# Four projections of a hybrid decoder layer as seven half products in place of eight, with the sums of two on GpSimd

## What is computed

```python
x += W_out[concat(NSA heads, GLA heads)](RMSNorm(x) @ W_in)   # NSA: 8 query heads, 2 key/value heads, 3 branches
q = rms_norm(q.reshape(B, S, NSA_HEADS, dh), q_norm_g)        # each head of 64 is normed
q_rot = apply_partial_rope(q, positions)                      # the first 16 features of each head are turned
o = (o_intra + o_inter); o = rms_norm(o, norm_g)              # GLA: 4 heads, values of width 128
return (o * jax.nn.silu(r)).astype(q.dtype)                   # r: the GLA gate
x += MoE(RMSNorm(x))                                          # top 4 of 32 experts, 1024 -> 2048 -> 1024 each
```

## Time and profile before

| | before |
|---|---|
| median of 3 runs | 1060.35 us (1059.74 to 1060.77) |
| span of the profiled execution | 1056.8 us |
| median less span | 3.55 us |
| TensorE busy | 1015.2 us (96%) |
| VectorE, ScalarE, GpSimd busy | 311.4, 167.2, 15.8 us |
| TensorE's waits in the first 160 us | 3.3 us |
| memory read | 424.83 MB, 403 GB/s over the span |

### The profile page before, as it was taken

One profiled execution on the slowest core, in us unless ns is written; L12 is line 12 of the kernel. 1 busy time (PEld: TensorE's weight loads), 2 busy tenths in 40 slices (PEclk: granted clock), 3 DMA queues, 4 the chain that ended last, 5 costly groups with the idle time before them and its releaser, 6 DMA issues.

```text
span 1056.8 us, 12109 instructions
## 1 busy us (share of the span) xinstructions
PE 1015.2 (96%) x4965; PEld 409.4 (39%) x4965; DVE 311.4 (29%) x711; ACT 167.2 (16%) x324; POOL 15.8 (1%) x42
## 2 busy tenths in 40 slices
PE   9999999999999999999999999999999999999998
PEld 6555654333333333333233333333333333333333
DVE  1666675222212222222222222222112221222222
ACT  2433422111101111111011001111111110111111
POOL 4100000000000000000000000000000000000000
PEclk9999999999999999999999999999999999999999
DMA  9992599999999999999999999999999999999997
GB/s 293 361 381 85 215 368 378 419 426 432 431 430 429 433 433 426 433 433 433 432 429 433 434 432 429 432 434 432 429 434 433 430 429 431 431 432 429 422 424 288
DMA packets 37187, 426.37 MB, mean 403 GB/s; under 512 B 3927, under 2 KB 12207, under 8 KB 20513
## 3 DMA queue, kind: packets, MB, share of 16 engines
q1 hardware_dynamic: 35120, 424.52, 95.8%
q0 software_dynamic: 704, 1.04, 0.5%
q10 hardware_dynamic: 1328, 0.33, 0.1%
HBM read 424.83 MB, written 1.05 MB: 403 GB/s over the span
## 4 chain that ended last, share of the span: by engine, by line
PE 66%; DMA 30%; DVE 2%; issue 1%; ACT 0%; SPq 0%; DVEq 0%
PE bank L1859 26%; DMA pair<-in_w_down 26%; PE bank L1871 15%; PE bank L1426 5%; DMA pair<-in_w_gate_up 4%; PE bank L1893 4%; PE bank L1835 3%; PE bank L1701 2%; PE bank L1885 2%; PE bank L1843 1%; PE bank L1878 1%; PE bank L1498 1%; PE bank L2095 1%; PE bank L1458 1%; PE bank L1485 1%; PE bank L1468 1%
## 5 line engine op out<-in xcount | busy, mean ns | idle before, releaser
L1859 PE MATMUL bank<-pair,xs 128*64 128x512 f32 x2032 | 446.3, 594 | 20.3 <-DMA pair<-in_w_gate_up 19.2
L1859 PEld LDWEIGHTS bank<-pair,xs 128*64 128x64 f32 x2032 | 142.2, 137 | 319.1 <-issue 286.0
L1871 PE MATMUL bank<-pair,sig 128*64 128x512 f32 x960 | 212.4, 594 | 13.3 <-DMA pair<-in_w_down 13.3
L1319 DVE COPY gu<-bank 128x512 f32<-128x512 f32 x32 | 36.3, 1134 | 413.9 <-PE bank L1859 413.9
L1871 PEld LDWEIGHTS bank<-pair,sig 128*64 128x64 f32 x960 | 72.4, 137 | 149.1 <-issue 143.7
L794 ACT COPY gu<-bank 128x512 f32<-128x512 f32 x32 | 36.2, 1133 | 457.7 <-PE bank L1859 457.7
L903 DVE TENSOR_TENSOR xs<-bank,gt 128x512 f32<-128x512 f32 x31 | 21.4, 691 | 220.5 <-PE bank L1843 220.5
L1426 PE MATMUL bank<-stage,xt 128*128 128x512 f32 x160 | 72.2, 598 | 0.0
L1893 PE MATMUL bank<-ys,pgt 64*128 64x512 f32 x248 | 61.6, 615 | 0.0
L1835 PE MATMUL bank<-xr,onehot 128*64 128x512 f32 x248 | 58.5, 592 | 0.0
L799 ACT COPY ys<-bank 128x512 f32<-128x512 f32 x31 | 18.1, 585 | 206.4 <-PE bank L1871 206.4
(11 more groups left out here) (338 smaller groups left out, 524.9 us busy)
## 6 DMA issues: line engine op xcount, KB each, us to landing
pair<-in_w_gate_up SPq DMA_DIRECT2D x51, 4096.0 KB, 40.9
pair<-in_w_down SPq DMA_DIRECT2D x24, 4096.0 KB, 38.9
pair<-in_w_gate_up SPq DMA_DIRECT2D x20, 2048.0 KB, 12.8
pair<-in_w_down SPq DMA_DIRECT2D x18, 1024.0 KB, 12.2
stage<-in_w_in SPq DMA_DIRECT2D x5, 2048.0 KB, 19.0
pair<-in_w_down SPq DMA_DIRECT2D x4, 2048.0 KB, 31.0
pair<-in_w_gate_up SPq DMA_DIRECT2D x8, 1024.0 KB, 7.6
stage<-in_w_out SPq DMA_DIRECT2D x2, 2048.0 KB, 13.4
```

The lines of the kernel that those rows point to most:

```text
L1319: V.tensor_copy(gu[:, 1, :].rearrange("p (i q) -> p q i", i=FQ), up_banks[1][:].rearrange("p (q i) -> p q i", i=FQ)).then_inc(s["gu_lo"], 1)
L1859: last = mm(up_banks[a][b * CAP:(b + 1) * CAP, :].rearrange("p (q i) -> p q i", i=FQ), xs[:, k, :], cols[:, b], start=k == 0, stop=k == DK ...
L1871: last = mm(down_bank[b * CAP:(b + 1) * CAP, :], actf[:, kk % FQ, kk // FQ, :], row[:, 512 * b:512 * (b + 1)], start=kk == 0, stop=kk == D ...
```

## The change

1. **Seven half products.** For q, kv, gv and gr the two tiles and two halves of 512 columns are treated as a 2x2 block product. With x11, x12 (tile 0, features 0-511 and 512-1023), x21, x22 (tile 1), and the quarters b11, b12, b21, b22 of the weights, seven products of half the depth and half the width are taken in the order 1, 2, 6, 5, 7, 3, 4 (`seventh(m, i)`): four matmuls with 256 moving columns each. Before, the two tiles took sixteen matmuls of 512 columns.
2. **Sums of x.** `xsum` holds four sums of blocks of x, made once by VectorE.
3. **Sums of weights.** Four tensor-tensor operations of 128x1024 for each of the four pieces, two of them written over the weights in their slot. VectorE makes them for q and kv (`seventh_sum`), GpSimd for gv and gr (`pool_sum`).
4. **Copies and joins.** ScalarE copies the banks behind products 1, 6, 5, 4 (`part_out`); VectorE adds the banks behind products 2, 7, 3 into the copied rows (`join`), since product 2 and its followers are shared by two results.
5. **Order.** q now comes before kv. The heads of both tiles are normed together, once for q's eight heads and once for the four key heads, and turned together. `hidden` runs as a whole behind half of gqk. Several tables of VectorE move behind the turning of heads.
6. **Loads.** Four small loads (`brow`) move behind the other small ones that TensorE and VectorE wait for. A load of 1 MB of expert weights (`kept_half(extra, KEPT[0], 1)`) moves from behind the first half of W_out to behind the load that waits for gr to be complete, since `extra` now holds `xsum` and the sums.

```diff
-PROJ = [("w", 1024, 280), ("kv", 512, 512), ("q", 0, 512), ("gqk", 1304, 512), ("gv", 1816, 512), ("gr", 2344, 512)]
+PROJ = [("w", 1024, 280), ("q", 0, 512), ("kv", 512, 512), ("gqk", 1304, 512), ("gv", 1816, 512), ("gr", 2344, 512)]
+SEVEN_ORDER = (1, 2, 6, 5, 7, 3, 4)
+COPIED = (1, 6, 5, 4)
+JOINED = (2, 7, 3)
@@ SyncE
-                if i == NF - 2:
-                    kept_half(extra, KEPT[0], 1)
...
             front_used(sp, 7)
             rows_in_place(1, 0, 1, 2, 4, "ring1")
+            kept_half(extra, KEPT[0], 1)
             sp.wait_ge(s["o_full"], 1)
@@ GpSimd
+            def pool_sum(m, t):
+                b11, b12, b21, b22 = quarters_of(m)
+                one, two = (r[:] for r in sum_rooms[m])
+                if t == 4:
+                    seventh_done(pool, m, 2)
+                dst, a, b = {1: (one, b12, b11), 3: (b12, b22, b12), 2: (two, b22, one), 4: (b21, b21, two)}[t]
+                step(nc.gpsimd.tensor_tensor(dst, a, b, ALU.subtract))
+
+            front_arrived(pool, LOADS.index(("in", PGV)))
+            seventh_done(pool, PKV, 5)
+            summed(pool, PKV, 4)
+            for t in (1, 3, 2):
+                pool_sum(PGV, t)
+            pool.wait_ge(s["qr_full"], 3)
+            front_arrived(pool, LOADS.index(("in", PGR)))
+            pool_sum_order = ((PGV, 4), (PGR, 1), (PGR, 3), (PGR, 2), (PGR, 4))
@@ ScalarE
+            def part_out(m, i):
+                ti, half = tile_and_half(i)
+                seventh_done(act, m, i)
+                for dst, src in landing(m, i):
+                    last = nc.scalar.activation(dst, src, ACT.Copy, scale=rs_x[:, ti:ti + 1])
+                last.then_inc(s["proj"], 1)
@@ VectorE
+            def join(m, i):
+                ti, half = tile_and_half(i)
+                seventh_done(dve, m, i)
+                copied(dve, m, {2: 1, 7: 5, 3: 6}[i])
+                for dst, src in landing(m, i):
+                    last = V.scalar_tensor_tensor(out=dst, in0=src, scalar=rs_x[:, ti:ti + 1], in1=dst,
+                                                  op0=ALU.mult, op1=ALU.add)
+                last.then_inc(s["joined"], 1)
...
+            seventh_sum(PKV, 4)
+            join(PKV, 2)
+            norm_heads(0, HQ)
+            join(PKV, 7)
+            join(PKV, 3)
@@ TensorE
+            def seventh(m, i):
...
+                elif i == 6:
+                    weights_summed(m, 2)
+                    copied(pe, m, 1)
+                elif i == 5:
+                    weights_summed(m, 1)
+                    if m in (PGV, PGR):
+                        joined(pe, m, 2)
+                elif i == 7:
+                    weights_summed(m, 3)
+                    copied(pe, m, 6)
+                elif i == 3:
+                    summed(pe, "x", 4)
+                    copied(pe, m, 5)
+                elif i == 4:
+                    weights_summed(m, 4)
+                    joined(pe, m, 7)
+                one, two = sum_rooms[m]
+                left, right = {1: (x11, b11), 2: (x12, b21), 3: (xsum[:, 3], b22), 4: (x22, b21), 5: (xsum[:, 0], one),
+                               6: (xsum[:, 1], two), 7: (xsum[:, 2], b12)}[i]
+                for k in range(4):
+                    last = mm(bank_part(m, i), left[:, k, :], right[:, k, :], start=k == 0 and i in (1, 2, 5), stop=k == 3,
+                              skip_group_check=True)
...
-            project(10, 1)
+            seventh(PGR, 5)
             pe.wait_ge(s["ats"], 2)
             turned(3)
-            project(11, 0)
+            seventh(PGR, 7)
```

More of the change, by code:

```diff
@@ L5 @@
 from contextlib import ExitStack
+from itertools import accumulate
 F32 = mybir.dt.float32
@@ L561, in _ @@
             ]
-            small += [(brow[E * q:E * (q + 1), :, :], b_gate_up[0].rearrange("e (a c) -> e a c", a=2)[:, :, 256 * q:256 * (q + 1)])
-                      for q in range(4)]
-            late = [
+            late = [(brow[E * q:E * (q + 1), :, :], b_gate_up[0].rearrange("e (a c) -> e a c", a=2)[:, :, 256 * q:256 * (q + 1)])
+                    for q in range(4)] + [
                 (w2[:, 0, :, :], split_k(cmp_w2_k[0])),
@@ L686, in _ @@
                                  scale=1.0 / GTAU).then_inc(s["dec"], 1)
-            act.wait_ge(s["proj"], 2)
-            nc.scalar.activation(gsig, gt[:, :, 0:24], ACT.Tanh, scale=0.5).then_inc(s["gsg"], 1)
+            part_out(PKV, 4)
+            act.wait_ge(s["kx_full"], 1)
+            kvt = banks[3][:].rearrange("p (c t i) -> p c t i", c=2, i=2)
+            for i in range(2):
+                for h in range(HKV):
+                    nc.scalar.copy(kx[i * DH:(i + 1) * DH, :, h, :], kvt[h * DH:(h + 1) * DH, :, :, i])\
+                        .then_inc(s["kx"], 1)
             for ti in range(NT):
@@ L935, in _ @@
+            for t in (1, 3, 2):
+                seventh_sum(PQ, t)
+            seventh_sum(PQ, 4)
+            join(PQ, 2)
             dve.wait_ge(s["rows_full"], 1)
             dve.wait_ge(s["small"], 16 * N_SMALL)
+            posf = rope[:, 4, 0, 0:NT]
+            link(V.tensor_copy(posf, poss[:]))
+            link(V.tensor_tensor(rope[:, 0, :, :], bc(posf, RD // 2),
+                                 invf[:].unsqueeze(1).to_broadcast([P, NT, RD // 2]), ALU.mult))
+            link(V.tensor_scalar(rope[:, 1, :, :], rope[:, 0, :, :], 1 / (2 * math.pi), MAGIC, ALU.mult, ALU.add))
@@ L937, in _ @@
+            link(V.tensor_scalar(rope[:, 1, :, :], rope[:, 1, :, :], -MAGIC, None, ALU.add))
+            for c in TWO_PI:
+                link(V.scalar_tensor_tensor(out=rope[:, 0, :, :], in0=rope[:, 1, :, :], scalar=-c,
+                                            in1=rope[:, 0, :, :], op0=ALU.mult, op1=ALU.add))
+            V.tensor_scalar(rope[:, 0, :, :], rope[:, 0, :, :], PI32, -PI32, ALU.min, ALU.max).then_inc(s["rope"], 1)
+            join(PQ, 7)
             heads = vecs[:, 0:4 * DH].rearrange("p (b d) -> p b d", d=DH)
@@ L960, in _ @@
[L960 to L967 removed]
+            join(PQ, 3)
@@ L1085, in _ @@
             weigh(1)
+            join(PGV, 2)
             soft(2)
@@ L1101, in _ @@
             weigh(4)
+            join(PGR, 7)
             soft(5)
@@ L1113, in _ @@
                 dve.wait_ge(s["sta"], 2 * ci + 1)
+            join(PGR, 3)
             weigh(5)
@@ L1410, in _, with project @@
                     tp(banks[4][:, 0:DK], grows[:], ident[0:DK, 0:DK]).then_inc(s["g1_full"], 1)
[L1412 to L1425 removed]
+            def project(n, first, end):
+                m, ti = n // NT, n % NT
+                width = PROJ[m][2]
+                if first == 0:
+                    front_arrived(pe, LOADS.index(("in", m)))
+                    copied(pe, PQ, 4)
+                    joined(pe, PQ, 3)
+                for k in range(first, end):
@@ L1426, in project, with weights_summed @@
                     last = mm(banks[PROJ_BANKS[n]][:, 0:width], xt[:, k, ti * P:(ti + 1) * P],
-                              front_slot(LOADS.index(("in", piece)))[:, k, 0:width], start=k == 0, stop=k == DK - 1)
-                if part != 0:
+                              front_slot(LOADS.index(("in", m)))[:, k, 0:width], start=k == 0, stop=k == DK - 1)
+                if end == DK:
                     last.then_inc(s["proj_full"], 1)
+            def weights_summed(m, t):
+                if m in (PQ, PKV):
+                    summed(pe, m, t)
+                else:
+                    pool_summed(pe, m, t)
@@ L1529, in _ @@
             last.then_inc(s["post_full"], 1)
-            project(5)
+            for i in (1, 2, 6, 5, 7):
+                seventh(PKV, i)
             pe.wait_ge(s["loga"], 1)
@@ L1540, in _ @@
             last.then_inc(s["decay_full"], 1)
+            seventh(PKV, 3)
+            seventh(PKV, 4)
+            pe.wait_ge(s["tables"], 1)
+            joined(pe, PKV, 3)
+            for c in range(2):
+                for ti in range(NT):
+                    last = tp(banks[3][:, (2 * c + ti) * P:(2 * c + ti + 1) * P], kv[:, ti, c * P:(c + 1) * P], ident[:])
+            last.then_inc(s["kx_full"], 1)
             pe.wait_ge(s["rn"], 1)
-            pe.wait_ge(s["proj"], 5)
-            heads_turned(0, banks[4], "qt_full")
+            copied(pe, PKV, 4)
+            for ti in range(NT):
+                heads_turned(ti, banks[4 + ti], "qt_full")
+            project(6, 0, 4)
             for c in range(2):
```

355 lines of the change are left out of this document (207 added, 148 removed).

## The result

The change made the kernel slower. Its median is 1064.46 us (1063.10 to 1065.35, 5 executions) beside 1059.74 us (1057.36 to 1060.77) of the kernel before: a ratio of 1.0048, 95% interval 1.0038 to 1.0059. Measured again beside eleven executions of before, 1063.38 to 1058.76, it was 1.0045 (1.0032 to 1.0059). So the change costs 4.6 to 4.7 us. I had forecast 4.7 us less, and a range whose upper end, 1062.6, the time passed. Ratios and medians here leave out one execution, of the kernel of experiment 6, that took twice the time.

A forecast was written before the change was run, and what follows sets the result against it. TensorE bounds the front, memory the rest. Gains of 2.6 us (q, kv) and 2.1 us (gv, gr) sum to 4.7 us, giving 1055.6 us; the forecast's own range is 1054 to 1057, the full range 1053.8 to 1062.6.

The forecast's parts named there:

- VectorE may as well win each turn: Head norming, 52.0 to 58.3 us: GpSimd's sums would not hold up VectorE, whose steps follow in 0.03 us; forecast's chance 0.48.
- Rival 1: Head norming, 52.0 to 58.3 us: GpSimd's sums shut VectorE out, time 1058.2 to 1062.4 us; chance 0.32.
- GpSimd's price: Duration p of one GpSimd weight sum of 1024 elements: lower bound 1.06 us, upper bound 2.1 us, 2.1 taken.
- 3p - 0.7: TensorE's wait at the turned heads if three GpSimd sums each shut VectorE out for p, less 0.7 us margin.
- as long as before: `hidden`, ahead of the turned heads on TensorE: costed at 3.76 us, unchanged.
- q and kv: Front, 17.66 to 63 us: first scores 2.6 us earlier, from 3.44 + 0.5 - 1.0 - 0.3.
- the kv join: TensorE at product 4 of kv waits about 1.0 us for VectorE's join, ready at 44.6 us.
- the copy: Head transposes wait 0.3 us for ScalarE's copy of the bank product 4 of kv has just filled.
- gv and gr: Behind GLA's scores: two savings, 3.44 us, less a 1.3 us TensorE wait for `ats`, bring 2.1 us.
- The 3.55 us: Whole kernel: the median of the runs lies 3.55 us above the span, turning 1052.1 into 1055.65 us.
- The end follows the front: Expert weights' stream starts earlier when TensorE comes through the front earlier; the end moves one for one.
- The moved load: Load of 1.05 MB into the DMA pause at 124 to 128 us: costed at nothing, 2.4 us as other bound.

The follow-up runs named there:

- experiment 6: Changed kernel with only the hidden layer split in two: 1065.06 us, ratio 1.0056; and kernel before with its hidden layer in one row: 1058.22 us, ratio 0.9999.
- experiment 1: Kernel before with three unused GpSimd subtractions of 128x1024 added once the value weights land: 1066.96 us, ratio 1.0086.
- experiment 2: Kernel before with three GpSimd memsets of 128x2048 added once the value weights land: 1058.63 us, ratio 1.0003.
- first profile: Changed kernel's first profiled execution: 51.17 us from first q or kv product to first scores (A), 66.00 us on to the output product (B); series median 1064.46 us.
- second profile: Same changed kernel profiled again: 48.74 us from first q or kv product to first scores, 66.00 us on to the output product; series median 1063.38 us.
- experiment 3: Changed kernel with GpSimd's first three value-weight sums moved behind the turned heads: 1060.38 us, ratio 1.0015.
- experiment 5: Changed kernel with GpSimd's first sums behind the turned heads and the hidden layer in two halves: 1059.41 us, ratio 1.0008.
- the mended order: Changed kernel with GpSimd's first sums behind the heads, its last gate sums later, and joins, `ats` and GLA's scores reordered: 1056.89 us, ratio 0.9987.
- experiment 7: Changed kernel with GpSimd's sums later and joins, `ats` and GLA's scores reordered: 1056.89 us; with the hidden layer split as well: 1055.50 us.
- Experiment 9: Changed kernel with gv and gr back at eight half products: 1060.14 us; with hidden layer split and gr's banks as before: 1056.01 us, ratio 0.9991.
- the fastest: The mended order with hidden layer split, all eight gv and gr sums on VectorE and join 7 of gv moved: 1053.64 us, ratio 0.9954.

## Why the prediction was wrong

**The step that failed** is the choice of the likeliest case: "VectorE may as well win each turn", with 0.48 for the forecast and 0.32 for Rival 1. Rival 1 is what happened, in its place, by its mechanism and nearly with its price. The argument for the forecast was that VectorE's steps follow each other in 0.03 us. But in the trace VectorE is held to the end of GpSimd's operation, so GpSimd needs to win only once per sum. It won all three times: at 51.56, 54.05 and 56.49 its sum began while a step of VectorE was under way that still took 0.17 us, and the next step was held. That it comes up in one of the gaps is my reading of these times. The rows of before spoke for neither view, and I let the milder one stand first without a row that showed it. The Trainium skill's "SBUF — State Buffer", section "SBUF: two separate sides", says that whichever starts first has the ports for the whole instruction; experiments 1 and 2 agree, with 2.26 us for a step of 0.17 beside a subtraction and 0.17 beside a memset.

**GpSimd's price.** I had taken 2.1 us as the upper bound; measured were 2.35 to 2.46 (one 3.06). The bound came from the slope of two selects with one input and was called a bound without a reason; it should have been open above. The Trainium skill's "GPSIMD Engine Reference", section 3.1, has 4497 ns for 2048 elements; half of it, an estimate of 2.25 us, is 5% under the trace. Of Rival 1's formula 3p - 0.7 = 6.4 us the trace has 5.5: one sum costs VectorE 2.04 us, its duration less the time until VectorE next needs SBUF.

**A term that was missing: the clock.** No rival had it. 5.5 us of wait brought 2.5 us more at half clock. With it the first profile's sum is 4.7 - 5.5 - 2.5, less 0.9 for the longer wait for `ats` and 1.1 for the gv join: -5.3 us, where its distances say -5.7. The second profile's say -3.3, and the medians, between the two, -4.6 to -4.7.

**A second term that was missing: the stop.** That `hidden` runs as a whole I had costed "as long as before". In most profiles it goes with a stop of 2.0 us, which the wait for the heads hid in the changed kernel and which stood in the open once that wait was gone. Shortening it was worth about 1 us of median from experiment 3 to 5 and 1.4 in the mended order, neither clear of noise. Why the kernel before has no such stop stays open.

**q and kv: right, where no stop falls.** Forecast 2.6 us; distance A of experiment 5 is 45.92 - 43.34 = 2.58 us less. In its execution no stop came; in those of experiments 7 and 9 with the hidden layer split, which have one, A is 2.1 and 1.3 us less. By the steps: the kv join waits 0.55 and not 1.0 us, the copy 0.37 (0.3), eight records of a half product lie 1.72 us apart, and TensorE comes to the heads 0.8 us after they are ready in the changed kernel had there been no lock (57.03 against 62.38 - 6.12 = 56.26; forecast 0.7). Experiment 9 has 2.7 us of median, with the wide interval. The agreement to the tenth is in part luck: the two waits are 0.4 us shorter together than I had them, so some 0.4 us was lost elsewhere, and I don't know where. Two slips in the prediction's text change little: the steps in a row on VectorE are 28 and not 24, and its terms for the turned heads add up to 56.1 and not 56.3, a margin of 0.8 us, as measured.

**gv and gr: size off.** Forecast 2.1 us less in B, measured 0.45 more. TensorE waited 2.2 us for `ats`, not 1.3. Two of GpSimd's sums hold VectorE ahead of it: `weigh(2)` takes 3.38 us in place of 1.22, and the second group of sums for W_out 4.26 in place of 2.49. Rival 1 had only the second of these. And the gv join, of which I had said that each user stands two products behind, waited 1.1 us, since VectorE was then behind with the softmax. The mended order brings 1.3, with the sums on VectorE 1.7 of the 2.1.

**What lies around a span.** The 3.55 us were the median of three executions less the span of one whose own time isn't given. Where an execution has both, its time is 1.7 to 2.3 us above its span. The forecast isn't moved by this, since 4.7 us less than the median of before, 1060.35, is the same 1055.6.

**The end follows the front: right.** In the changed kernel A and B grew by 5.7 and 3.3 us in the two profiles and the median by 4.7; in the fastest they shrank by 4.8 and the median by 5.1. **The moved load** was hidden: 124 to 128 us, with 213 and 8 GB/s in the earlier trace rows, now carries 442 GB/s, and TensorE waits at 120 to 170 us only the 0.6 us for ScalarE's copy `ot`, as before.

## What to carry to other kernels

"Another engine is idle, give it the work" holds only if the two don't shut each other out: here, ahead of the turned heads, a sum took GpSimd 2.36 us and VectorE, which was to be relieved, 2.04 us of standing still, more than the 1.22 us of doing it itself. Before moving an operation to GpSimd, look at what VectorE does beside it and what waits for that, and put it where VectorE works out of PSUM or waits. And a wait of several microseconds on TensorE can cost more than itself: price the clock behind it, and look for what the wait had been hiding before you trust the gain from removing it.

## What the runs showed of the hardware

- The clock falls after idle stretches, but not always: 1.00 behind a stop of 2.04 us in experiment 7, 0.54 behind one of 2.02 us in experiment 3, both profiles of nearly the same program. After waits of 5.5 us (the changed kernel) and 6.6 us (experiment 1) it was 0.50. The spread of executions goes with it: in experiment 3 1056.15 us with a granted clock of 0.999 over the whole execution, and 1062.82 with 0.995.
- VectorE operations that read one of two operands from PSUM were not held: the two mask additions at 62.60 to 63.89 us in the split kernel of experiment 7 took 1.29 us together, as in the kernel before, beside a sum of GpSimd at 62.28 to 64.63. A small one with a single input was held: 1.92 us for a TENSOR_SCALAR of eight elements, 0.17 elsewhere. The Trainium skill's "SBUF — State Buffer", section "Who interferes with whom", names tensor_scalar among those that can take the shared ports, and leaves out operations with one SBUF input otherwise; both rows agree.
- It works the other way too: a select of GpSimd of 128x128, 0.29 us in the earlier trace rows, took 0.98 us in the changed kernel while VectorE summed weights.
